# A hybrid decode step on one core: x scaled tile by tile, constants fetched later, index keys and head weights as one unit of 80 columns

## What is computed

```
xn = RMSNorm(x);  z = xn @ w_in         # q | k | v | index q | index k (64) | head weights (16) | conv | gate A | gate B
s  = relu(iq . ik / 8) summed over 16 heads with weights iw   # lightning indexer
attention over the top-k keys by s, with T5 relative bias
conv branch; h = x + (sig(gA) A + sig(gB) B) @ w_out;  h + SwiGLU(RMSNorm(h))
```

## Time and profile before

| | us |
|---|---|
| median of 3 runs (lowest, highest) | 2187.06 (2183.96, 2192.33) |
| the profiled execution | 2192.3 |
| its span | 2190.8 |
| PE busy | 2088.3 (95%) |
| DVE, ACT, POOL busy | 1236.1, 905.7, 152.5 |
| mean granted clock | 0.97 |

### The profile page before, as it was taken

One profiled execution on the slowest core, in us unless ns is written; L12 is line 12 of the kernel. 1 busy time (PEld: TensorE's weight loads), 2 busy tenths in 40 slices (PEclk: granted clock), 3 DMA queues, 4 the chain that ended last, 5 costly groups with the idle time before them and its releaser, 6 DMA issues.

```text
span 2190.8 us, 40585 instructions
## 1 busy us (share of the span) xinstructions
PE 2088.3 (95%) x14615; PEld 1972.3 (90%) x14615; DVE 1236.1 (56%) x2261; ACT 905.7 (41%) x1648; POOL 152.5 (7%) x284
## 2 busy tenths in 40 slices
PE   5959999979998999999999999999999999999997
PEld 5944899859998777899999999999999999999997
DVE  4413898626666799884564455554455554445553
ACT  5512444324444333435544455543344443344443
POOL 4300000011111221000000000000000000000012
PEclk9969999869999899999999999999999999999999
DMA  8450346327876799454654455555555555555574
GB/s 223 104 109 20 101 130 169 102 83 231 242 239 205 238 318 313 126 154 126 194 153 134 134 154 152 146 145 151 153 153 146 145 150 154 152 145 145 151 202 115
DMA packets 549653, 350.99 MB, mean 160 GB/s; under 512 B 19298, under 2 KB 528522, under 8 KB 549167
## 3 DMA queue, kind: packets, MB, share of 16 engines
q1 hardware_dynamic: 522672, 264.08, 44.8%
q0 software_dynamic: 25792, 84.46, 12.1%
q10 hardware_dynamic: 1088, 1.05, 0.1%
HBM read 339.43 MB, written 10.83 MB: 160 GB/s over the span
## 4 chain that ended last, share of the span: by engine, by line
PE 66%; DVE 1%; ACT 0%; issue 0%; POOL 0%; DVEq 0%; POOLq 0%; ACTq 0%
PE psG L1346 20%; PE psG L1347 20%; PE psG L1348 20%; PE psS L1343 2%; PE psM L1348 1%; PE psM L1347 1%; PE psM L1346 1%; PE psM L1343 1%; PE psM L1340 0%; PE psG L1340 0%; DVE stat L1169 0%; DVE OL L1228 0%; ACT L L742 0%; PE psT L1340 0%; DVE L L1164 0%
## 5 line engine op out<-in xcount | busy, mean ns | idle before, releaser
L906 DVE TENSOR_TENSOR WL<-RAW,WH 128x512 fp32r<-128x512 f32 x1000 | 674.6, 688 | 693.2 <-ACT WH L540 691.4
L540 ACT ACTIVATE WH<-RAW 128x512 fp32r<-128x512 f32 x1000 | 618.9, 628 | 900.1 <-PE psG L1348 814.4
L1346 PE MATMUL psG<-XH,WH 128*128 128x320 f32 (+1 forms) x2688 | 847.5, 315 | 3.1 <-DVE WL L906 2.1
L1347 PE MATMUL psG<-XL,WH 128*128 128x320 f32 (+1 forms) x2688 | 837.4, 312 | 0.0
L1348 PE MATMUL psG<-XH,WL 128*128 128x320 f32 (+1 forms) x2688 | 835.3, 311 | 0.0
L1346 PEld LDWEIGHTS psG<-XH,WH 128*128 128x128 f32 x2688 | 506.2, 188 | 35.2 <-issue 31.3
L1347 PEld LDWEIGHTS psG<-XL,WH 128*128 128x128 f32 x2688 | 506.3, 188 | 1.2
L1348 PEld LDWEIGHTS psG<-XH,WL 128*128 128x128 f32 x2688 | 506.8, 189 | 0.0
L1346 PE MATMUL psG<-MH,WH 128*128 128x320 f32 x960 | 301.2, 314 | 0.3 <-DVE ML L1315 0.3
L1348 PE MATMUL psG<-MH,WL 128*128 128x320 f32 x960 | 296.6, 309 | 0.0
L1347 PE MATMUL psG<-ML,WH 128*128 128x320 f32 x960 | 296.5, 309 | 0.0
(11 more groups left out here) (339 smaller groups left out, 1758.3 us busy)
## 6 DMA issues: line engine op xcount, KB each, us to landing
RAW<-in_w_in SPq DMA_DIRECT2D x160, 512.0 KB, 5.3
RAW<-in_w_ffn_down SPq DMA_DIRECT2D x96, 512.0 KB, 4.7
RAW<-in_w_ffn_gate SPq DMA_DIRECT2D x88, 512.0 KB, 4.7
RAW<-in_w_ffn_up SPq DMA_DIRECT2D x88, 512.0 KB, 4.7
kst<-in_cache_k POOLq DMA_DIRECT2D x64, 512.0 KB, 4.4
vst<-in_cache_v POOLq DMA_DIRECT2D x64, 512.0 KB, 5.9
RAW<-in_w_out SPq DMA_DIRECT2D x32, 512.0 KB, 5.0
RAW<-in_w_attn_br SPq DMA_DIRECT2D x16, 512.0 KB, 4.7
```

What stands on the lines that cost most here:

```text
L540: act.activation(WH[:, s % 2, 4 * r:4 * r + 4, c], RAW[:, s, 4 * r:4 * r + 4, c], ACT.Copy).then_inc(hi_done, 1)
L906: dve.tensor_tensor(WL[:, s, k, c], RAW[:, s, k, c], WH[:, s % 2, k, c].bitcast(F32), ALU.subtract).then_inc(lo_done, 1)
L1346: pe.matmul(out, WH[:, s % 2, k], hi, start=start, stop=False)
L1347: pe.matmul(out, WH[:, s % 2, k], lo, start=False, stop=False)
```

## The change

Loads of x count on three semaphores, and ACT squares each tile as it lands. ACT scales tiles 0 and 1 to a new buffer `xs`, POOL scales tile 2; DVE inverts the root after five of the raw copies instead of 13. POOL loads the page table and the small parameters first and issues the seven other constants behind the first eight pages. The table products, with the transposes of `w_dw`, move behind the fourth `iq` unit, and DVE's copies ahead of its split of the ninth. Index keys and head weights become one unit of 16 tiles and 80 columns; the other three units of the group stay in the counting as zero copies and 1x1 products. The key copy in partitions 64 to 127 is made by a DMA. PE does two quarters of the first `qk` unit before the set-up and two behind it, and the second unit's four quarters behind every eighth head product. New-key scores move behind the seventh total; head products go in pairs of heads.

```diff
-            sp.dma_start(xtok[:, 1, :], xp[P - N_META:2 * P - N_META]).then_inc(x_ld, 16)
-            sp.dma_start(xtok[0:N_META, 2, :], xp[2 * P - N_META:SEQ]).then_inc(x_ld, 16)
-            sp.dma_start(xtok[N_META:N_META + NS, 2, :], I["x_sample"].rearrange("b q d -> (b q) d")).then_inc(x_ld, 16)
+            sp.dma_start(xtok[:, 1, :], xp[P - N_META:2 * P - N_META]).then_inc(x1_ld, 16)
+            sp.dma_start(xtok[0:N_META, 2, :], xp[2 * P - N_META:SEQ]).then_inc(x2_ld, 16)
+            sp.dma_start(xtok[N_META:N_META + NS, 2, :], I["x_sample"].rearrange("b q d -> (b q) d")).then_inc(x2_ld, 16)
...
-            for s in range(2):
-                w = w_in[:, 8 * s:8 * s + 8, C_IK:C_IK + ID]
-                load(G0["ikiw"], s, RAW[:, s, 0:8, 0:ID], w, RAW[:, s, 0:8, ID:P], w)
-            for s in range(2):
-                w = w_in[:, 8 * s:8 * s + 8, C_IW:C_IW + IH]
-                load(G0["ikiw"], 2 + s, RAW[:, 2 + s, 0:4, 0:IH], w[:, 0:4], RAW[:, 2 + s, 4:8, 0:IH], w[:, 4:8])
+            w = w_in[:, :, C_IK:C_IK + ID + IH]
+            load(G0["ikiw"], 0, RAW[:, 0, 0:8, 0:ID + IH], w[:, 0:8], RAW[:, 0, 8:KT, 0:ID + IH], w[:, 8:KT])
+            for s in range(1, 4):
+                sp.wait_ge(mm_done, 16 * G0["ikiw"] + (4 * s - 12))
+                sp.sem_inc(w_ld[s], 32)
...
-            small = [(oh[:], I["c_oh"]), (relx[0:BUCKETS, :], I["rel_bias"]),
-                     (wrow[:], I["w_dw"][0])]
+            pool.dma_start(ptab[:], I["page_table"].rearrange("b (o n) -> o (b n)", o=1)).then_inc(pt_ld, 16)
...
-                small.append((prow[r:r + n, :], I[name].rearrange("o (n p) -> (o n) p", p=P)))
-            for dst, src in small:
-                pool.dma_start(dst, src).then_inc(c_ld, 16)
-            for dst, src in ((ptab[:], I["page_table"].rearrange("b (o n) -> o (b n)", o=1)), (esel[:], I["c_esel"]),
-                             (qm[:], I["c_qm"]), (cms[:], I["c_cms"]), (cmp_[:], I["c_cmp"])):
-                pool.dma_start(dst, src).then_inc(c2_ld, 16)
-            pool.wait_ge(c2_ld, 80)
+                pool.dma_start(prow[r:r + n, :], I[name].rearrange("o (n p) -> (o n) p", p=P)).then_inc(c_ld, 16)
+            pool.wait_ge(pt_ld, 16)
...
+                if b == 0:
+                    pool.wait_ge(a_rms, 1)
+                    n = XTILES[2][1]
+                    pool.tensor_scalar(xs[0:n, 2, :], xtok[0:n, 2, :], stat[0:n, 10:11], None, ALU.mult).then_inc(a_xp, 1)
+                    for dst, src in ((oh[:], I["c_oh"]), (relx[0:BUCKETS, :], I["rel_bias"]), (wrow[:], I["w_dw"][0]),
+                                     (esel[64:64 + IH, :], I["c_esel"]), (qm[:], I["c_qm"]), (cms[:], I["c_cms"]), (cmp_[:], I["c_cmp"])):
+                        pool.dma_start(dst, src).then_inc(c2_ld, 16)
...
             pool.dma_start(gscr.ap(), gsb[:, None, :].to_broadcast([H, P, RELW])).then_inc(g_wr, 16)
+            for i in range(2):
+                pool.wait_ge(ev[i], 2 * (G0["ikiw"] + 1) + 1)
+            pool.dma_start(ikT[ID:2 * ID, :], ikT[0:ID, :]).then_inc(ik_dp, 16)
...
-            act.wait_ge(x_ld, 96)
...
             for i, (_, n) in enumerate(XTILES):
+                act.wait_ge((x_ld, x1_ld, x2_ld)[i], (48, 16, 32)[i])
...
             act.wait_ge(a_rms, 1)
-            act.wait_ge(a_tr, KT)
-            for i, (_, n) in enumerate(XTILES):
-                act.activation(xtok[0:n, i, :], xtok[0:n, i, :], ACT.Copy, scale=stat[0:n, 8 + i:9 + i]).then_inc(a_xs, 1)
+            for i, (_, n) in enumerate(XTILES[0:2]):
+                act.activation(xs[0:n, i, :], xtok[0:n, i, :], ACT.Copy, scale=stat[0:n, 8 + i:9 + i]).then_inc(a_xs, 1)
...
+            ahead(g, 0)
+            keys(6)
+            ahead(g, 1)
+            ahead(g, 2)
+            done(g, 0)
+            half = NT // 2
+            for i in range(2):
+                c = slice(half * i, half * i + half)
+                act.activation(ikT[0:ID, c], MB[0][0:ID, c], ACT.Copy).then_inc(ev[i], 1)
+            for i in range(2):
+                c = slice(half * i, half * i + half)
+                act.activation(iwT[ID:ID + IH, c], MB[0][ID:ID + IH, c], ACT.Copy, scale=2.0 ** -5).then_inc(ev[i], 1)
+            keys(7)
+            ahead(g, 3)
...
-                if k == 3 * KT // 4:
+                if k == KT // 4:
                     dve.wait_ge(a_sqrt, 1)
                     dve.reciprocal(stat[:, 8:11], stat[:, 4:7]).then_inc(a_rms, 1)
...
+            def tables():
+                dve.wait_ge(a_tab, 1)
+                dve.tensor_copy(wdw[:], MB[0][:, 0:CT * CW].rearrange("p (c w) -> p c w", c=CT))
+                dve.tensor_copy(gsb[:], SB[0][0:H, 0:RELW])
+                dve.tensor_copy(biasR[:, B_FAR:B_N], SB[0][:, RELW:RELW + 1])
+                for c in range(2):
+                    dve.tensor_copy(bT7[:, c], SB[1][:, 0:Q * H].rearrange("p (q h) -> p h q", q=Q))
+                    ins = dve.tensor_copy(bNw[:, c], SB[1][0:NS, P:P + Q * H].rearrange("p (q h) -> p h q", q=Q))
+                ins.then_inc(a_bias, 1)
+
             for u in range(4 * GN["iq"]):
                 if u >= 2:
                     keys(u - 2)
+                if u == 3:
+                    dve.wait_ge(c2_ld, 112)
+                    dve.tensor_copy(relb[:].rearrange("p c h q -> p h c q"), relx[:][:, :, None, None].to_broadcast([33, H, 2, Q])).then_inc(a_rel, 1)
+                if u == 6:
+                    tables()
...
             for s in range(4):
+                if s == 1:
+                    keys(6)
+                if s == 3:
+                    keys(7)
                 ahead(G0["ikiw"], s)
-                if s % 2 == 0:
-                    keys(6 + s // 2)
...
             for b in range(B):
                 dve.wait_ge(idx_mm, b + 1)
                 dve.tensor_scalar(rl[:, b % 2, 512:PAST], (SB, TB)[b % 2][1][:], 0.0, None, ALU.max).then_inc(d_rlD, 1)
+            dve.wait_ge(n_mm, 1)
+            dve.tensor_scalar(rln[:], SB[0][:, 0:NS], 0.0, None, ALU.max).then_inc(d_rln, 1)
             dve.wait_ge(sum_mm, B)
...
-                dve.tensor_copy(Ss[:, 512 * i:512 * i + 512], G[i][0:NS, :])
...
+                dve.tensor_copy(Ss[:, 512 * i:512 * i + 512], MB[i][0:NS, :])
+            dve.wait_ge(sum_mm, B + 1)
+            ch.link(dve.tensor_tensor(Ss[:, PAST:LS], TB[0][0:NS, 0:Q], cms[:], ALU.min))
...
-                h, qt = i // 2, i % 2
+                h, qt = 2 * (i // 4) + i % 2, i // 2 % 2
...
-            pe.wait_ge(c_ld, 160)
-            tr(G[0][:, 0:R_N], prow[:])
-            for c in range(CT):
-                ins = tr(G[1][:, CW * c:CW * c + CW], wrow[:, P * c:P * c + P])
-            ins.then_inc(a_par, 1)
-            pe.wait_ge(a_xs, 3)
+            pe.wait_ge(c_ld, 112)
+            tr(G[0][:, 0:R_N], prow[:]).then_inc(a_par, 1)
+            pe.wait_ge(a_xs, 2)
+            pe.wait_ge(a_xp, 1)
...
-                turn_x(xtok, k)
+                turn_x(xs, k)
...
-            pe.wait_ge(a_lo, KT)
-            mm(SB[0][0:H, 0:RELW], relx[:], oh[:, OH_G:OH_G + RELW])
...
-
...
+                if u == 3:
+                    pe.wait_ge(c2_ld, 112)
+                    for c in range(CT):
+                        tr(MB[0][:, CW * c:CW * c + CW], wrow[:, P * c:P * c + P])
+                    mm(SB[0][0:H, 0:RELW], relx[:], oh[:, OH_G:OH_G + RELW])
+                    for q in range(Q):
+                        mm(SB[1][:, H * q:H * q + H], oh[:, OH_T7 + P * q:OH_T7 + P * q + P], relx[:])
+                        mm(SB[1][0:NS, P + H * q:P + H * q + H], oh[:, OH_NEW + NS * q:OH_NEW + NS * q + NS], relx[:])
+                    pe.wait_ge(a_rel, 1)
+                    mm(SB[0][:, RELW:RELW + 1], relb[:].rearrange("p c h q -> p (c h q)"), oh[:, OH_FAR:OH_FAR + 1]).then_inc(a_tab, 1)
+
+            g = G0["ikiw"]
+            ready(g, 0)
             pe.wait_ge(a_bias, 1)
+
+            def product(k):
+                out, w = MB[0][0:ID + IH, 0:NT], slice(0, ID + IH)
+                pe.matmul(out, WH[:, 0, k, w], XH[:, k, :], start=k == 0, stop=False)
+                pe.matmul(out, WH[:, 0, k, w], XL[:, k, :], start=False, stop=False)
+                return pe.matmul(out, WL[:, 0, k, w], XH[:, k, :], start=False, stop=k == KT - 1)
+
+            products(g, 0, range(KT), KT, product)
+            keys(B - 1)
+            for s in range(1, 4):
+                pe.wait_ge(lo_done, 16 * g + (4 * s + 4))
+                mm(MB[1][0:1, 0:1], zer[0:1, 0:1], ones[0:1, 0:1]).then_inc(mm_done, 4)
+
+            for r in range(2):
+                x_quarter(G0["qk"], 0, r)
             pe.wait_ge(d_cpA, B)
             pe.wait_ge(d_cpD, B)
             for qt in range(2):
-                tr(TB[0][:, IH * qt:IH * qt + IH], iwT[:, T0C + P * qt:T0C + P * qt + P])
-            mm(TB[0][:, 2 * IH:2 * IH + NS], esel[:], iwT[:, NP:NT])
+                pe.transpose(TB[0][:, IH * qt:IH * qt + IH], iwT[ID:ID + IH, T0C + P * qt:T0C + P * qt + P], ident[ID:ID + IH, ID:ID + IH])
```

(36 more changed lines are left out.)

89 lines of the change are left out of this document (21 added, 68 removed).

## The result

| | before | changed |
|---|---|---|
| time, median of the runs | 2186.66 us (2183.96 to 2192.33, 4 runs) | 2173.23 us (2171.56 to 2179.28, 4 runs) |
| profiled execution: time / span | 2192.33 / 2190.8 us | 2179.28 / 2177.8 us |
| granted clock over the span | 0.970 | 0.965 |

The ratio is 0.9938, 95% interval 0.9919 to 0.9957: 13.4 us faster. Both profiled executions are the slowest of their four runs, and differ by 13.0 us.

The account below looks back on a forecast made before the run. PE, busy 95% of the span, was taken as the bound, waiting at the index stage behind the bias write. Restart at 140.2 instead of 156.46 gains 16.3, index stage 0: median 2171 us, range 2163 to 2183.

Parts of the forecast that it names:

- Start: 36: Opening: earlier squares and scaling win 5.4 us, x landing sooner 1; first product at 36 instead of 42.3.
- POOL: POOL's queue: scaling 2.5 us, eight pages 9.1; `xT_scratch` write issued at 36.5, POOL free for the bias write at 95.
- A new wait: 4 us: Index query units: PE idles 4 us for `ikb` behind `xT_scratch`; of 6.4 us won, 2.4 are left.
- no stall in iq: Rival: page table early and x 2 us sooner, so POOL's 95 decides; gain 20 to 24, 2165; chance 0.08.
- Tables, write at 98.7: Table products moved earlier: bias write issued at 98.7, 14 us earlier, bound by PE, landing at 133.6.
- Load behind the write: 136.8: q/k load issued at 119.5 meets the bias write for 14 us and lands 3.2 us after its end, at 136.8.
- All of that is hidden: 7.4 us: Index product: 7.4 us of PE work removed, all hidden because PE then waits anyway.
- One unit of 80 columns: Index keys and head weights: 96 products of 336 columns become 48, 7.4 us removed but counted as hidden.
- Index stage: 0: From restart to the stage's end, 72.2 us: work moved, not removed, counted 0 with ends -2 and +3.
- Slower: the clock falls in the head loop: Rival: fewer quarters in the head loop, half clock costs 22 us, 2193; decides at two thirds of loop; chance 0.07.
- The gain arrives whole: From 260 us on PE is busy 39.51 of 40 us, so what is gained before should arrive at the end whole.
- Head products overlap: Rival: paired heads in different partition halves run at once in the head loop; 6 us, 2165; chance 0.05.

Follow-up runs that it names:

- e1: Changed kernel with only the bias write held on POOL until the last of the eight query products is done: 2183.98 us, ratio 0.9977.
- e3: Changed kernel with the splitting of q/k units 0 and 1 moved into the score loop, unit 0's quarters back in the head loop: 2147.26 us.
- e7: Changed kernel with the head loop's old order put back, head by head with the two query tiles in turn: 2175.10 us, ratio 0.9933.
- e9: Changed kernel with 48 dead products of 80 and 336 columns added ahead of the index product: 2171.41 us, ratio 0.9918.
- e10: e3 with 48 dead products of 80 and 336 columns added ahead of the index product: 2149.37 us, ratio 0.9836.
- e11: e10 with 96 dead products instead of 48: 2166.60 us, ratio 0.9902.
- e12: The same edit as e3 on the changed kernel, run again: 2148.22 us, ratio 0.9818.
- b1: Kernel before, with only the bias table products and their copies moved early so the bias write may go out sooner: 2187.09 us, ratio 0.9992.
- e8: Changed kernel with the edits of e3 and e2 together, and the third scaling on ACT instead of POOL: 2147.43 us, ratio 0.9814.
- e2: Changed kernel with the bias write moved behind the three index key outputs: 2160.47 us, ratio 0.9871.
- b2: Kernel before, with only e3's move of the splitting of the first two q/k units into the score loop: 2163.46 us, ratio 0.9882.

## Why the prediction was right, point by point

The forecast was 2171, measured 2173.23, and the restart 140.2, measured 137.8. The path was right: the write held the q/k load, the load held ACT, and ACT held PE (e1). That the number came so close is in good part luck: terms that were wrong cancelled. Steps:

- *Start: 36.* Measured 35.47, out of two errors. x landed at 15.41, 2.6 us sooner and not 1. POOL's scaling took 5.48 us, not 2.5: outside the ends of 1.8 and 3.7 that I had drawn from the memset and from ACT. All nine profiles in which POOL does it show 5.47 or 5.48. The 4.4 that I had estimated from the Trainium skill (GPSIMD Engine Reference, Performance versus the Vector engine), and set aside, was nearer, though still too low. The row that I chose, a memset, reads nothing, and so was no neighbour. Its cost fell on PE's second transposes, that waited for it until 25.55.
- *POOL.* I charged eight pages behind the scaling at 9.1 us. They were issued in 4.2 (29.2 to 33.4), so `xT_scratch` went out at 33.39, not 36.5, in spite of the slow scaling.
- *A new wait: 4 us.* It didn't occur. The keys of the first page were ready at 49.5, when PE was still in its second unit (first key transposes 51.17, not 54.4). This was the second rival, "no stall in iq", whose 2165 was not reached, for the reason under the next point.
- *Tables, write at 98.7.* Measured 96.91, set by PE as said (POOL had waited 5.96 us for the tables), and landing 34.7 us later, as said. The nearness is luck: the clock took what the stall did not. From 36 to 94 us the mean granted clock was 0.88, which is 7.0 us of full speed lost, where I had counted 2.5. Up to the write, e3, e7, e9, e10, e11 and e12 run the same code, and it went out between 94.14 (e10, clock 0.94 there) and 98.41 (e3, 0.86):

```profile
36.00:94.00 58.00, 58.00 (x372) 56.69 (x371) 23.05 (x37) 27.14 (x54) 24.46 (x46) 0.88 0.55 153
```

- *Load behind the write: 136.8.* ACT had the unit at 134.84; the load was issued at 117.51, since the index product ended 2 us sooner than I had it. The mechanism stands, and e1 shows it one for one. (The printed terms add up to 140.0; 109 packets at the pace of 89 in 2.8 us take 3.4, not 3.2, and give the 140.2.) What did not hold is that both queues' packets pass about in turn all along, so that 19 of 128 are through when the write ends: the earlier trace rows shows only the end of the write before. From 126 to 130 us, in the changed kernel and before, q0 moved 43 and 41 packets and q1 none; from 132 to 134, behind the write, q1 moved 1088.
- *All of that is hidden: 7.4 us.* Shown by e9. But "One unit of 80 columns" was put down as worth nothing, and b1 shows that it isn't: not by its products but because its load is out of the way. The step named the cover, and missed that the removed loads were the next to collide.
- *Index stage: 0.* 156.46 to 230.57 is 74.1 us, 137.79 to 212.21 is 74.4. The 0 is a sum of things that I had not sized: a saving of the new order (2.7 us at full clock), less half clock before the loop (4.4 us instead of 10.9), and 13.7 us of half clock in the loop. With the quarters left in the loop (e3, e8, e10 to e12) the stage takes 69.1 to 69.7.
- *Slower: the clock falls in the head loop.* It did, for 13.7 of 31 us, less than the two thirds from which it was to decide, and one sign that I had named as proving me wrong came true: the loop took over 30 us (30.96). The mechanism of this rival, fewer quarters in the loop, is borne out by all 13 profiles (e3), and I had given it 0.07. Its price was too high: in e2 and e9 half clock does hold for two thirds of the loop, and the loop takes 35 us, 4 more than in the changed kernel.
- *The gain arrives whole.* It did not in the profiled pair (18.4 to 13.0), for the clock. That the forecast came within 2 us rests in part on this: my local gain was too small by 2.4 and I had no term for the 5.
- *Head products overlap.* They do (e7): PE's work falls by 5.6 us at full clock, near the 6 of the rival, and 2.7 reach the loop. I had given it 0.05. The Trainium skill (TensorE: Matmul & The Clock Gate, Part 3) says that matmuls in different row groups run concurrently, and the trace agrees: 1.42 us for what takes 2.18 with shared rows.

## What to carry to other kernels

A wait for a transfer has two ends. Before the transfer is moved or made faster, look at who stands in line behind the waiting instruction on its engine without needing the data: there, moving two units' splitting (b2) brought 23.7 us where the whole change brought 13.4. If a slow, narrow write is moved instead, list every load that is issued in the 35 us that it covers in its new place (b1), and try it later as well as earlier (e2). When dense work is moved out of a loop that has pauses, look at the loop's granted clock afterwards: here it was full in all eight profiles with eight quarters in the loop, and at half for a part in all five with four (e2, e3). And take the price of an operation that has no row from a row that reads as many inputs and runs on the same engine.
